# A retention stage whose decode chunk becomes the fifteenth of seventeen steps

## What is computed

```python
h = rms_norm(x, p['norm1_w']) * (1.0 + sc1) + sh1
proj = h @ p['w_in']                       # columns: retention q, k, v, gate; then mLSTM q, k, v, o, ...
q_r = rotary(_heads(rq, R_HEADS), pos)
k_r = rotary(_heads(rk, R_HEADS), pos) * (R_DK ** -0.5)

def step(S, inp):                          # prompt: 16 chunks of 128 tokens; decode: 1 chunk of 4 for each sequence
    qc, kc, vc = inp
    s = einsum('bhtd,bhsd->bhts', qc, kc) * inner
    o = einsum('bhts,bhse->bhte', s, vc) + einsum('bhtd,bhde->bhte', qc * qdec, S)
    S = cdec * S + einsum('bhsd,bhse->bhde', kc * kdec, vc)
    return S, o

y_r = head_norm(_merge(o_r), p['ret_norm_w'], R_HEADS) * silu(rg)
```

## Time and profile before

| what | us |
| --- | --- |
| runs: lowest, median, highest | 2697.43, 2701.71, 2702.18 |
| span of the profiled execution | 2697.6 |
| PE busy (share of the span) | 2461.4 (91%) |
| DVE busy | 1864.8 (69%) |
| ACT busy | 911.2 (34%) |
| POOL busy | 403.5 (15%) |
| DMA, mean | 108 GB/s |

### The profile page before, as it was taken

One profiled execution on the slowest core, in us unless ns is written; L12 is line 12 of the kernel. 1 busy time (PEld: TensorE's weight loads), 2 busy tenths in 40 slices (PEclk: granted clock), 3 DMA queues, 4 the chain that ended last, 5 costly groups with the idle time before them and its releaser, 6 DMA issues. The chain is left out here.

```text
span 2697.6 us, 44581 instructions
## 1 busy us (share of the span) xinstructions
PE 2461.4 (91%) x17104; PEld 1521.1 (56%) x17104; DVE 1864.8 (69%) x3831; ACT 911.2 (34%) x1383; POOL 403.5 (15%) x384
## 2 busy tenths in 40 slices
PE   3899999879989999599969999999999998889997
PEld 1455555567667786455536666666666663334443
DVE  4555555446888886578867777777767668787666
ACT  1433333214444444144432222222222224332222
POOL 0132322300000000012242212221222200000000
PEclk7999999989999999699989999999999999999999
DMA  7434443460242311333412221222122217543323
GB/s 260 154 106 140 160 144 109 141 204 21 86 159 102 132 55 38 114 125 108 133 45 74 80 75 49 73 79 75 50 78 73 75 47 237 183 145 106 106 86 94
DMA packets 209320, 291.36 MB, mean 108 GB/s; under 512 B 19727, under 2 KB 146239, under 8 KB 207027
## 3 DMA queue, kind: packets, MB, share of 16 engines
q1 hardware_dynamic: 208933, 289.72, 33.0%
q10 hardware_dynamic: 270, 0.10, 0.0%
HBM read 214.48 MB, written 75.29 MB: 107 GB/s over the span
## 5 line engine op out<-in xcount | busy, mean ns | idle before, releaser
L2586 PE MATMUL py<-h_parts,w_heads 128*128 128x384 f16 (+1 forms) x792 | 246.0, 311 | 19.6 <-DVE u_p L2741 19.6
L2587 PE MATMUL py<-h_parts,w_heads 128*128 128x384 f16 (+1 forms) x792 | 245.8, 310 | 0.0
L2588 PE MATMUL py<-h_parts,w_heads 128*128 128x384 f16 (+1 forms) x792 | 245.8, 310 | 0.0
L336 PE MATMUL prj<-w_heads,h_parts_t 128*128 128x512 f16 x512 | 195.8, 382 | 12.6 <-PEq L451 6.2
L337 PE MATMUL prj<-w_heads,h_parts_t 128*128 128x512 f16 x512 | 195.6, 382 | 0.0
L338 PE MATMUL prj<-w_heads,h_parts_t 128*128 128x512 f16 x512 | 195.3, 382 | 0.0
L336 PE MATMUL m_prj<-m_h,w_heads 128*128 128x128 f16 (+1 forms) x1088 | 179.1, 218 | 12.5 <-DMA m_h<-h_parts 11.2
L2586 PE MATMUL px<-h_parts,w_heads 128*128 128x384 f16 (+1 forms) x528 | 164.4, 311 | 17.5 <-PEq L1884 17.5
L337 PE MATMUL m_prj<-m_h,w_heads 128*128 128x128 f16 (+1 forms) x1088 | 179.1, 217 | 0.0
L338 PE MATMUL m_prj<-m_h,w_heads 128*128 128x128 f16 (+1 forms) x1088 | 179.0, 217 | 0.0
L2587 PE MATMUL px<-h_parts,w_heads 128*128 128x384 f16 (+1 forms) x528 | 164.5, 311 | 0.0
(11 more groups left out here) (553 smaller groups left out, 6022.6 us busy)
## 6 DMA issues: line engine op xcount, KB each, us to landing
C_new<-in_w_up_dram SPq DMA_DIRECT2D x11, 2048.0 KB, 7.6
w_heads<-in_w_up_dram SPq DMA_DIRECT2D x44, 512.0 KB, 5.5
d_a<-act_cols SPq DMA_DIRECT2D x174, 128.0 KB, 2.4
act_cols<-w_heads SPq DMA_DIRECT2D x44, 384.0 KB, 2.4
win_raw<-in_w_ada_dram SPq DMA_DIRECT2D x8, 2048.0 KB
first_a<-in_w_down_dram SPq DMA_DIRECT2D x22, 512.0 KB, 3.8
first_a<-in_w_down_dram SPq DMA_DIRECT2D x44, 256.0 KB, 3.4
wa<-in_w_ada_dram SPq DMA_DIRECT2D x4, 2048.0 KB, 11.3
```

The lines of the kernel that those rows point to most:

```text
L336: nc.tensor.matmul(out, left[0], right[0], start=(k == 0), stop=False)
L2586: nc.tensor.matmul(out, left[0], right[0], start=(start and k == 0), stop=False, skip_group_check=True)
L2587: nc.tensor.matmul(out, left[0], right[1], start=False, stop=False, skip_group_check=True)
L2588: last = nc.tensor.matmul(out, left[1], right[0], start=False, stop=(k == KC // 2 - 1), skip_group_check=True)
```

## The change

The decode chunk is moved from place 17 to place 15. In the changed code `DEC` = 14 is the decode chunk's step and `LAST` = 16 the last step, so steps 0 to 13 are prompt chunks 0 to 13, step 14 is decode, and steps 15 and 16 are prompt chunks 14 and 15 (`chunk`, `row`, `rows`, and `prompts` turn step numbers into chunks, rows and counts). The three last steps of the loop of 12 are written out. On PE, after step 13, come `turn_x(15)`, `project_decode(14)`, and the rest of step 13; then step 15 with the decode chunk's transposes, scores and outputs in it (`decode_outputs`), and the products for the 8 states in pairs (`state_products`): the first pair at the end of step 15, the others between the four projections of step 16. DVE makes new states between its other work in the same order. v, the gate and the decayed k of the decode chunk have tiles of their own (`v_d`, `g_d`, `kd_d`), and so have the masked queries (`qm`).

The weight tile is laid out quarter by quarter, so that a quarter is one piece of 16 KB in each partition, and SP requests each mLSTM quarter when the last step's projection with the retention quarter in its place is done (`load_mls`). The two halves of the output projection's weights are laid out and loaded in the same way (`wide`).

```diff
-    core.w_heads = core.heads[:].rearrange("p (i k n) -> p i k n", i=2, k=KC)
+    core.w_heads = core.heads[:].rearrange("p (q i k n) -> p q i k n", q=4, i=2, k=KC)
...
+                             + [(win[:, :, q * W:(q + 1) * W], w[:, q, 0], w[:, q, 1]) for q in range(4)],
...
+        v_d, g_d, kd_d, qm = sb("v_dec", [NS, H, HD]), sb("gate_dec", [NS, W]), sb("k_decayed_dec", [NS, H, HD]), sb("q_masked", [P, H, DB, NS])
...
+        DEC, LAST = NCH - 2, NCH
+        rows = lambda c: NS if c == DEC else P
+        chunk = lambda c: c - (c > DEC)
+        row = lambda c: SEQ if c == DEC else chunk(c) * P
+        prompts = lambda c: c - 1 if isinstance(c, int) and c > DEC else c
+        bank_of = lambda b: flat_tpx[:, (b % 2) * 512:(b % 2 + 1) * 512]
...
-            step(NCH - 5)
+            def late_loads(c):
+                load_rope(c + 1, rows(c + 1), row(c + 1))
+                sp.wait_ge(s["h_lo"], c + 2)
+                at = NCH if c + 1 == DEC else chunk(c + 1)
+                sp.dma_start(core.h1[at][:, :, :, 0:rows(c + 1)], h[:, :, :, 0:rows(c + 1)]).then_inc(s["h_saved"], 16)
+                if c + 2 <= LAST:
+                    norm.load_x(sp, io["x_sample"].rearrange("b s n -> (b s) n") if c + 2 == DEC else x_rows[chunk(c + 2)], c + 2, rows(c + 2))
+
+            def save_rows(c):
+                sp.wait_ge(s["y_here"], c + 1)
+                sp.dma_start(core.y[row(c):row(c) + rows(c), 0:W], y[0:rows(c)].rearrange("p h e -> p (h e)")).then_inc(s["y_saved"], 16)
+
+            def save_state(b):
+                sp.wait_ge(s["sb_here"], b + 1)
+                sp.dma_start(io["ret_s"][0, b].rearrange("h d e -> d h e"), S_new[:, b]).then_inc(s["s_saved"], 16)
+
+            def load_mls(q):
+
+                sp.wait_ge(s[("q_done", "k_done", "v_done", "g_done")[q]], NCH)
+                sp.dma_start(w[:, q], core.wp_mls[q]).then_inc(core.w_mls_in[q], 16)
+
+            late_loads(DEC - 3)
+            save_rows(DEC - 4)
             save_late(LATE - 2, 0)
             load_late(LATE - 1, 1)
-            step(NCH - 4)
+            late_loads(DEC - 2)
+            save_rows(DEC - 3)
             save_late(LATE - 1, 1)
-            step(NCH - 3)
+            late_loads(DEC - 1)
+            save_rows(DEC - 2)
             prep.store_parts(sp, 3)
-            load_rope(NCH - 1, P, (NCH - 1) * P)
-            save_h(NCH - 1, P)
-            norm.load_x(sp, io["x_sample"].rearrange("b s n -> (b s) n"), NCH, NS)
-            save_y(NCH - 3, P)
-            load_rope(NCH, NS, SEQ)
-            save_h(NCH, NS)
-            save_y(NCH - 2, P)
+            late_loads(DEC)
+            save_rows(DEC - 1)
+            late_loads(DEC + 1)
+            save_rows(DEC)
             sp.wait_ge(prep.parts_free, 16 * 5)
             sp.wait_ge(s["dec_done"], 1)
-            for q in range(4):
-                sp.dma_start(w[:, :, :, q * W:(q + 1) * W], core.wp_mls[q]).then_inc(core.w_mls_in[q], 16)
-            save_y(NCH - 1, P)
+            save_state(0)
+            save_state(1)
+            load_mls(0)
+            load_mls(1)
+            save_state(2)
+            save_state(3)
+            load_mls(2)
+            save_state(4)
+            save_state(5)
+            load_mls(3)
+            save_state(6)
+            save_state(7)
+            save_rows(LAST - 1)
+            save_rows(LAST)
             sp.wait_ge(s["state_here"], NCH)
             sp.dma_start(io["ret_p"][0, 0].rearrange("h d e -> d h e"), S[:]).then_inc(s["s_saved"], 16)
-            for b in range(DB):
-                if b == DB - 2:
-                    save_y(NCH, NS)
-                sp.wait_ge(s["sb_here"], b + 1)
-                sp.dma_start(io["ret_s"][0, b].rearrange("h d e -> d h e"), S_new[:, b]).then_inc(s["s_saved"], 16)
             sp.wait_ge(s["s_saved"], 16 * (1 + DB))
...
+                if q == 0 and isinstance(c, int) and c == DEC + 1:
+                    pe.wait_ge(s["v_here"], c)
+                    pe.wait_ge(s["g_tanh"], c)
...
+            def decode_outputs(c):
+
+                pe.wait_ge(s["v_here"], c + 1)
+                pe.wait_ge(s["probs_here"], c + 1)
+                pe.wait_ge(s["qm_here"], 1)
+                pe.wait_ge(s["state_in"], 16)
+                for i in range(H):
+                    out = att[0:NS, 1, i * P:(i + 1) * P]
+                    for e in range(DB):
+                        pe.matmul(out, qm[:, i, e, :], S_s[:, e, i, :], start=(e == 0), stop=False)
+                    last = pe.matmul(out, pr[0:NS, i, 0:NS], v_d[:, i, :], start=False, stop=True)
+                last.then_inc(s["o_done"], 1)
+
+            def state_products(first):
+
+                pe.wait_ge(s["v_here"], DEC + 1)
+                for b in (first, first + 1):
+                    if b < 2:
+                        pe.wait_ge(s["h_full"], LAST + 1)
+                    else:
+                        pe.wait_ge(s["sb_here"], b - 1)
+                    pe.wait_ge(s["km_here"], b + 1)
+                    for i in range(H):
+                        last = pe.matmul(bank_of(b)[:, i * P:(i + 1) * P], km[:, b % 2, i, :], v_d[:, i, :], start=True, stop=True)
+                    last.then_inc(s["sb_done"], 1)
...
-            step(NCH - 2, P, P, P, None, LATE)
-            step(NCH - 1, P, P, NS)
-            last_step(NCH, P)
...
+            step(DEC - 3, P, P, P, LATE - 2, LATE - 2)
+            step(DEC - 2, P, P, P, LATE - 1, LATE - 1)
+            step(DEC - 1, P, P, NS, None, LATE)
+            turn_x(DEC + 1, P)
+            project_decode(DEC)
+            turn_qk(DEC - 1, P)
+            scores(DEC - 1, P)
+            outputs(DEC - 1)
+            c = DEC + 1
+            project(0, c, P)
+            project(1, c, P)
+            turn_qk(DEC, NS)
+            turn_x(LAST, P)
+            project(2, c, P)
+            scores(DEC, NS)
+            project(3, c, P)
+            decode_outputs(DEC)
+            state_products(0)
+            project(0, LAST, P)
+            state_products(2)
+            project(1, LAST, P)
+            turn_qk(LAST - 1, P)
+            state_products(4)
+            project(2, LAST, P)
+            scores(LAST - 1, P)
+            state_products(6)
+            project(3, LAST, P)
+            outputs(LAST - 1)
+            pe.wait_ge(s["qk_rot"], LAST + 1)
+            pe.wait_ge(s["sb_here"], DB)
...
+            pe.wait_ge(s["state_here"], NCH - 1)
+            scores(LAST, P)
+            pe.wait_ge(s["y_here"], LAST)
+            outputs(LAST)
...
+                if isinstance(c, int) and c == DEC + 1:
+                    act.wait_ge(s["dec_done"], 1)
+                act.wait_ge(s["g_done"], prompts(c))
...
+            step(DEC - 3, P, P, P, P, qs_p)
+            step(DEC - 2, P, P, P, NS, qs_p)
+            step(DEC - 1, P, P, NS, P, qs_p, lambda: prep.cut_hi(act, 3))
+            h_full(DEC + 1, P)
+            h_hi(DEC + 1, P, True)
+            copy_qkT(DEC - 1, P)
+            decode_qk(DEC)
+            decode_v_gate(DEC)
+            norm.square(act, LAST, P)
+            step(DEC + 1, P, NS, P, 0, qs_p)
+            step(LAST, P, P, 0, 0, qs_p)
+            act.wait_ge(s["qk_turned"], LAST + 1)
+            act.wait_ge(s["o_done"], LAST)
+            nc.scalar.copy(qkT, tpx[:]).then_inc(s["qkT_here"], 1)
...
+            h_lo(DEC + 1, P)
+            probs(DEC - 1, P, mask_p)
+            state(DEC - 1)
+            norm_y(DEC - 1, P, steps)
+            rotate(DEC, NS, steps)
+            gate(DEC, NS)
+            norm.norm(dve, LAST, P)
+
+            rotate(DEC + 1, P, steps)
+            mask_queries()
+            dve.wait_ge(s["kd_here"], DEC + 1)
+            mask_k(0)
+            mask_k(1)
+            probs(DEC, NS, mask_s)
+            h_lo(LAST, P)
+            norm_y(DEC, NS, steps)
+            gate(DEC + 1, P)
+
+            for b in range(4):
+                new_state(b)
+            rotate(LAST, P, steps)
+            new_state(4)
+            new_state(5)
+            probs(LAST - 1, P, mask_p)
+            new_state(6)
+            new_state(7)
+            state(LAST - 1)
+            norm_y(LAST - 1, P, steps)
+            gate(LAST, P)
+            probs(LAST, P, mask_p)
+            state(LAST)
+            norm_y(LAST, P, steps)
...
-                sp.dma_start(wide[:, :, :, q * 512:(q + 1) * 512], core.wp_out[q]).then_inc(s["saved"], 16)
+                sp.dma_start(wide[:, q], core.wp_out[q]).then_inc(s["saved"], 16)
```

More of the change, by code:

```diff
@@ L1178, in _ @@
             step(1, P, P, P, dec_p)
-            with pool.Fori(0, 4) as b:
+            with pool.Fori(0, 3) as b:
                 step(3 * b + 2, P, P, P, dec_p)
@@ L1341, in project_cols @@
                     for k in range(KC):
-                        a = q * W + i * HD
-                        last = three_passes(nc, prj[:, (QB, KB)[q], i * P:i * P + T], [w[:, j, k, a:a + HD] for j in range(2)],
```

(1 more changed line is left out.)

140 lines of the change are left out of this document (48 added, 92 removed).

## The result

The changed kernel took 2711.95 to 2720.51 us in four runs, median 2715.25, against 2701.94 for four runs of the kernel before. Over all nine the median is 2716.6; the 109 runs of the kernel before that went beside all these have 2700.8. So the change costs 13 to 18 us, 15.8 by these two. The forecast was 7.4 us slower. The side was right, and 2715.25 lies in the range at its upper end; the size is about double, and that the time still lies in the range is owed to the room left there for rival C's longer waits, of which only a part came.

What follows compares the result with a forecast made beforehand. PE's matmuls bound the stage up to the decode projection's end, then a chain of small steps. Terms of 95.9 plus a tail of 24.8 give 120.7 against 113.3, 7.4 us slower: 2709.1 us, range 2701 to 2716.

Steps and rivals of the forecast that it cites:

- rival C: At the waits and restarts: low clock lasts longer and x lands some 2.5 us later; +13, 2714.6 us, chance 0.16.
- first wait: PE directly after step 13 waits for xn of chunk 15 (place in the order), 9.2 us.
- transposes, decode projection, restart: PE behind the first wait: transposes 0.88, decode projection 5.36, one clock restart 1.9, together 8.1 us.
- finishing chunk 13: After the decode projection: scores start 2.1 us later, then scores 0.88, mask 0.7, outputs 2.67, together 6.4 us.
- second wait: PE at the rows of step 16: rows take 16.1 us, PE has 10.8 of work, so it waits 5.3.
- to the end of the first state pair: After the second wait: transposes, restart 1.9, two projections, decode scores, four heads, two state products; 24.5 us.
- tail: From the end of chunk 14's products (the last prompt but one) to the first mLSTM matmul: 24.8 us.
- From there on everything is shifted: From the first mLSTM matmul on, later stages only start 7.4 us later; the span would be 2705.0 us.
- A (the clock holds): At the two waits the clock stays up, so no restarts; +1.5, 2703.2 us, chance 0.14.
- B (rows in time): At steps 15 and 16 both waits fall away, winning 12.7 us; -5.3, 2696.4 us, chance 0.12.
- D (weights late): At the mLSTM stage's start, weights arrive late; at 140 GB/s 8 us more, 2717 us, chance 0.03.
- What costs nothing: Weight loads and layout: last quarter requested some 27 us ahead against 6 needed; no matmul's shape changes, no cost.

Runs made afterwards that it cites:

- e4: The changed kernel with the last chunk's x load requested earlier and the decode projection ahead of chunk 14's transposes, ACT and DVE reordered to match; 2703.45 us, ratio 1.0016.
- e11: e4 plus decode copies ahead of chunk 14's modulation, a separate bank for the last outputs, earlier mask and state store; 2698.89 us, ratio 0.9999.
- e7: The changed kernel with 41 and 28 matmuls without use ahead of the two transposes that wait; 2708.63 us, ratio 1.0031 to before.
- e1: The kernel before with only the new quarter-by-quarter weight layout, order of work unchanged; 2701.22 us, ratio 1.0004 to before.
- e9: The kernel before with its mLSTM stage put off by four stores that SP waits for; 2712.13 us, ratio 1.0044.
- e12 to e14: The kernel before with its mLSTM stage put off by 2, 6 and 9 stores that SP waits for; 2705.85, 2714.23 and 2720.82 us.
- e16: The changed kernel with 33 matmuls without use behind PE's last of the retention stage; 2711.22 us, ratio 1.0036 to before.
- e10: The changed kernel in its order of work, with the weight layout of before; 2718.22 us, ratio 1.0067 to before.

## Why the prediction was half right

Its terms against the first profile after, which has 124.3 from the same start:

| term of the sum | forecast | measured |
| --- | --- | --- |
| first wait | 9.2 | 9.05 |
| transposes, decode projection, restart | 8.1 | 8.24 |
| finishing chunk 13 | 6.4 | 6.93 |
| two projections, decode transposes | 10.8 | 11.13 |
| second wait | 5.3 | 6.38 |
| to the end of the first state pair | 24.5 | 25.31 |
| step 16 | 31.6 | 31.75 |
| tail | 24.8 | 25.54 |

- **The mechanism** in the stretch was right: a wait for xn directly behind step 13's products, a second at the next rows, each with a low clock behind it. e4 and e11 take most of the waits away and e7 the low clock behind them, and the stretch falls each time. The profile after met the prediction's signs: 9.05, 6.38, a tail of 25.5, no wait on weights; the first mLSTM matmul came at 586.6 for 583.
- **The sum of the stretch** was 3.2 to 3.7 short. Largest: the second wait (+1.1), where x's load, issued behind table and h, took 501.23 - 495.59 = 5.6 us to its square and not 4.1 (why isn't shown: before, it was issued behind a save of h as well); and the second restart, 2.75 and not 1.9, which is nearly all of the +0.8 in the next term.
- **The step that failed** is the last: "From there on everything is shifted". It put the loss of the stages behind at nothing, on the ground that nothing differs there but the layout of weights; by the runs some 5 us more are lost outside the stretch (15.8 against 11.0), a third of the loss. With the 3.2 to 3.7 of the stretch this makes the loss about double the 7.4 forecast. Layout (e1) is not its cause, nor, as far as four delays can tell, is lateness (e9, e12 to e14); e16 takes it away, and its cause stays open.
- **Rivals.** A (the clock holds) fell by the windows above. B (rows in time) did not come by itself; e4 got rid of most of both waits by another order, and won 13.9 in the stretch where B had 12.7. C has its sign right: x lands late and one restart is longer, though only 2 us of its 5.6 came so; that its 2714.6 is so near the measured 2715.25 is luck. D (weights late) did not come: no PE wait on them, and e10 with the layout of before is equal.
- **What costs nothing**, layout and weights, cost nothing: e1.
- Four pairs of state products took 2.05, 2.31, 2.05 and 2.05 us, 8.5 in all, for 8.6 by the row of before. The Trainium skill, TensorE: Matmul & The Clock Gate, "Why this matters for your kernels", has a single matmul over 32 rows take as long as one over 128, by which the estimate was 7.1; the trace still disagrees: from 527.36 to the next matmul, at 529.34, eight such matmuls took 0.25 us each, where those over 128 rows took 0.22.

Behind the waits of 9.05 and 6.38 us the granted clock stood at 0.50. The Trainium skill, same page, section "HAM oscillation — how this bites in real kernels", says that long waits between bursts of matmuls put the clock down anew each time, and advises to order the loops so that PE stays at work. The trace agrees, at 1.9 and 2.75 us a time.

## What to carry to other kernels

When a short step is put between long ones, look at what the long step gave time for: here 10 us of projections covered the next rows' load and scaling, and a projection of 5.4 us that needs none of these rows stood behind the transposes that wait for them. Remove such waits together, since one hides the other, and count a restart of the clock for each that is left. Take no gain or loss at a stage's end over to the program's end unchecked: a shift of the stages behind should be measured by a plain delay.

## What the runs showed that was not expected

- 33 matmuls without use ahead of a stage boundary were worth 5 us in two kernels (2698.89 to 2693.95, 2716.6 to 2711.22). In a third (2701.42 against 2701.56) they won some 2.5 us behind the boundary and lost as much by making the next stage late.
- The same instructions from the first mLSTM matmul on took 2121.7 to 2132.0 us in the profiles. The largest part of it lies in the down stage, whose products take 436.5 to 442.6 us from first to last; in the longest, 2132.0, that stage also began 1667.4 us behind the first mLSTM matmul, for 1661.9 in the first profile of before.
- Two waits of 9.05 and 6.38 us gave 4.7 and 3.5 us in the stretch when treated one by one, and 13.9 together.
